# State updates of a gated linear attention, two chunks side by side in the row halves of the array

## The reference

```python
def step(S, inp):
    qn, kn, vn, gn = inp
    b = jnp.cumsum(gn, axis=1)
    b_last = b[:, -1]
    q_dec = qn * jnp.exp(b)
    k_inv = kn * jnp.exp(-b)
    attn = jnp.where(causal, jnp.einsum('bthd,bshd->bhts', q_dec, k_inv), 0.0)
    o = (jnp.einsum('bhts,bshv->bthv', attn, vn)
         + jnp.einsum('bthd,bhdv->bthv', q_dec, S))
    k_tail = kn * jnp.exp(b_last[:, None] - b)
    S = S * jnp.exp(b_last)[..., None] + jnp.einsum('bshd,bshv->bhdv', k_tail, vn)
    return S, o
```

## Time and profile before

| what | value |
|---|---|
| median of 3 runs | 4279.65 us (4272.71 to 4283.12) |
| the profiled execution | 4281.71 us |
| its span, first to last instruction | 4279.9 us |
| mean granted TensorE clock | 0.967 of full speed |
| the stage of the change, layer 0 and layer 1 | 116.98 and 113.94 us |

### The profile page before, as it was taken

One profiled execution on the slowest core, in us unless ns is written; L12 is line 12 of the kernel. 1 busy time (PEld: TensorE's weight loads), 2 busy tenths in 40 slices (PEclk: granted clock), 3 DMA queues, 4 the chain that ended last, 5 costly groups with the idle time before them and its releaser, 6 DMA issues.

```text
span 4279.9 us, 49995 instructions
## 1 busy us (share of the span) xinstructions
PE 4056.3 (95%) x18106; PEld 3279.2 (77%) x18106; DVE 2821.2 (66%) x4282; ACT 1530.1 (36%) x2219; POOL 1845.6 (43%) x956
## 2 busy tenths in 40 slices
PE   6899998998999999999998999989899999999999
PEld 4666876886877887888876668778778778788887
DVE  3124754698988946888733156247988989378786
ACT  2434523343333333333335255233333333333332
POOL 2321223344444446777423212333344444487772
PEclk9998989999999999999999998999999999999999
DMA  6434975243445459999934358463334544699996
GB/s 246 143 116 145 329 268 201 81 143 113 170 158 201 167 206 333 382 347 349 314 127 140 103 200 301 158 194 106 125 128 179 189 159 169 239 373 372 351 350 210
DMA packets 411891, 918.72 MB, mean 215 GB/s; under 512 B 38544, under 2 KB 176560, under 8 KB 410064
## 3 DMA queue, kind: packets, MB, share of 16 engines
q1 hardware_dynamic: 328080, 664.83, 44.8%
q0 software_dynamic: 45056, 134.38, 8.6%
q10 hardware_dynamic: 38592, 117.46, 7.0%
HBM read 793.85 MB, written 256.90 MB: 246 GB/s over the span
## 4 chain that ended last, share of the span: by engine, by line
PE 77%; issue 10%; DVE 6%; ACT 3%; POOL 3%; DMA 1%; SPq 1%; POOLq 0%; ACTq 0%; DVEq 0%
PE ps L887 13%; PE ps L888 13%; PE ps L889 13%; PE ps L902 10%; PE ps L903 10%; PE ps L904 10%; POOL w_lo L841 3%; PE ps L1185 2%; PE ps L1074 1%; PE ps L1059 1%; PE ps L1019 1%; DMA raw<-in_stream_dram 1%; ACT w_hi L519 1%; DVE raw L1263 1%; PE ps L1082 1%
## 5 line engine op out<-in xcount | busy, mean ns | idle before, releaser
L841 POOL TENSOR_TENSOR w_lo<-raw,w_hi 128x1024 fp32r<-128x1024 f32 x440 | 1133.5, 2577 | 2076.0 <-ACT w_hi L519 2076.0
L519 ACT ACTIVATE w_hi<-raw 128x1024 fp32r<-128x1024 f32 x504 | 534.2, 1060 | 1873.0 <-PE ps L889 1397.2
L887 PE MATMUL ps<-h_hi,w_hi 128*128 128x512 f32 x2880 | 1146.0, 398 | 7.9 <-DVE idxT L1522 7.8
L888 PE MATMUL ps<-h_hi,w_lo 128*128 128x512 f32 x2880 | 1137.3, 395 | 0.0
L889 PE MATMUL ps<-h_lo,w_hi 128*128 128x512 f32 x2880 | 1134.8, 394 | 0.0
L887 PEld LDWEIGHTS ps<-h_hi,w_hi 128*128 128x128 f32 x2880 | 550.3, 191 | 130.7 <-issue 17.4
L889 PEld LDWEIGHTS ps<-h_lo,w_hi 128*128 128x128 f32 x2880 | 547.8, 190 | 120.1
L888 PEld LDWEIGHTS ps<-h_hi,w_lo 128*128 128x128 f32 x2880 | 549.0, 191 | 107.9
L854 POOL DMA_INDIRECT down<-expert_down,e_row x256 | 336.3, 1314 | 216.6 <-DVE ps L1647 95.9
L1594 DVE TENSOR_TENSOR hot_i<-same_i,pick 128x1024 fp32r<-128x1024 f32 x192 | 421.5, 2195 | 0.0
L846 POOL DMA_INDIRECT acts<-expert_act,e_act x256 | 375.5, 1467 | 104.1 <-issue 77.4
(11 more groups left out here) (255 smaller groups left out, 6048.2 us busy)
## 6 DMA issues: line engine op xcount, KB each, us to landing
raw<-in_stream_dram SPq DMA_DIRECT2D x648, 512.0 KB, 3.4
expert_down<-in_stream_dram SPq DMA_DIRECT2D x256, 512.0 KB, 5.9
expert_act<-gel ACTq DMA_DIRECT2D x256, 256.0 KB, 2.0
raw_more<-in_stream_dram SPq DMA_DIRECT2D x128, 512.0 KB, 6.8
expert_gate<-gatebuf ACTq DMA_DIRECT2D x12, 4096.0 KB, 12.5
a_in<-expert_act SPq DMA_DIRECT2D x128, 384.0 KB, 6.6
g_in<-expert_gate SPq DMA_DIRECT2D x128, 384.0 KB, 8.2
ada_first<-in_stream_dram SPq DMA_DIRECT2D x16, 512.0 KB, 12.6
```

Source lines behind the costliest of these rows:

```text
L519: return act.activation(o, i, ACT.Copy)
L841: pool.tensor_tensor(w_lo[:, s, :], raw[:, b, :], w_hi[:, s, :].bitcast(F32), ALU.subtract).then_inc(lo_ready, 1)
L887: pe.matmul(o, w_hi[:, s, w], mov_hi[:, c, :], start=c == 0, stop=False)
L888: pe.matmul(o, w_lo[:, s, w], mov_hi[:, c, :], start=False, stop=False)
```

## The change

The updates of both chunks of a pair are made together, two heads at a time. The first half of a pair's updates (`half` 0) takes heads 0 and 1, the second heads 2 and 3. Within a half the order is head by head and, for each head, chunk `2 * p` in rows 0 to 63 and then chunk `2 * p + 1` in rows 64 to 127. The even chunk's products go to bank 4, the odd one's to bank 5. The last pair has only its even chunk. The unit stands between the two halves.

VectorE makes both halves before it waits for the squares. Since the odd chunk's state is now there before the pair's outputs have read the other two, a third state buffer is used, `state_2`, over the part of `grow` that is free in this stage.

```diff
+    state_2 = at("state_2", 88.5, [P, GH, DV])
...
+        def state_at(c, h):
+
+            return state[:, c % 3, h, :] if c % 3 < 2 else state_2[:, h, :]
...
+                def updates(l, p, half):
+                    n = l * 2 * TT + 2 * p + half
+                    if n:
+                        pe.wait_ge(state_ready, n)
+                    for h in (2 * half, 2 * half + 1):
+                        for e in range(2 if p < TT - 1 else 1):
+                            r = slice(64 * e, 64 * e + 64)
+                            mm = pe.matmul(ps[:, 4 + e, h % 2 * 256:h % 2 * 256 + 256], ktail[r, h, p, :],
+                                           v_g[r, p, h * DV:(h + 1) * DV], start=True, stop=True)
+                    mm.then_inc(upd_mm, 1)
...
-                    for e in range(2):
-                        c = 2 * p + e
-                        if e:
-                            unit(l, U_SQ + 3 * p)
-                        if c == 7:
-                            break
-                        if c:
-                            pe.wait_ge(state_ready, l * 7 + c)
-                        r = slice(64 * e, 64 * e + 64)
-                        for h in range(GH):
-                            mm = pe.matmul(ps[:, 4 + h // 2, h % 2 * 256:h % 2 * 256 + 256], ktail[r, h, p, :],
-                                           v_g[r, p, h * DV:(h + 1) * DV], start=True, stop=True)
-                        mm.then_inc(upd_mm, 1)
+                    updates(l, p, 0)
+                    unit(l, U_SQ + 3 * p)
+                    updates(l, p, 1)
...
-                    pe.wait_ge(state_ready, l * 7 + 2 * p + 1)
+                    pe.wait_ge(state_ready, l * 2 * TT + 2 * p + 2)
...
+                def update(p, half):
+                    dve.wait_ge(upd_mm, l * 2 * TT + 2 * p + half + 1)
+                    if p:
+                        dve.wait_ge(o_mm, l * TT + p)
+                    for e in range(2 if p < TT - 1 else 1):
+                        c = 2 * p + e
+                        for h in (2 * half, 2 * half + 1):
+                            u = ps[:, 4 + e, h % 2 * 256:h % 2 * 256 + 256]
+                            if c == 0:
+                                ins = dve.tensor_copy(state_at(1, h), u)
+                            else:
+                                ins = dve.scalar_tensor_tensor(out=state_at(c + 1, h), in0=state_at(c, h),
+                                                               scalar=small[:, 40 + h * 8 + c:41 + h * 8 + c], in1=u,
+                                                               op0=ALU.mult, op1=ALU.add)
+                        if e == 0 and p < TT - 1:
+                            step(ins)
                     ins.then_inc(state_ready, 1)
...
-                    update(2 * p)
+                    update(p, 0)
+                    update(p, 1)
                     dve.wait_ge(o_sq, l * 16 + 4 * (p + 1))
...
-                    if p < TT - 1:
-                        update(2 * p + 1)
```

More of the change, by code:

```diff
@@ L1033, in _ @@
                         if p:
-                            pe.matmul(o[0:64], q_g[:, h, t0:t0 + 64], state[:, 0, h, :], start=False, stop=False,
+                            pe.matmul(o[0:64], q_g[:, h, t0:t0 + 64], state_at(2 * p, h), start=False, stop=False,
                                       skip_group_check=True)
-                        mm = pe.matmul(o[64:128], q_g[:, h, t0 + 64:t0 + 128], state[:, 1, h, :], start=False, stop=True,
+                        mm = pe.matmul(o[64:128], q_g[:, h, t0 + 64:t0 + 128], state_at(2 * p + 1, h), start=False, stop=True,
                                        skip_group_check=True)
@@ L1323, in _ @@
                 mask = const[:, C_CAUSAL:C_CAUSAL + P].bitcast(U32).unsqueeze(1).to_broadcast([P, GH, P])
[L1325 to L1340, removed]
+                def update(p, half):
[14 more added lines that the diff above has]
+                            step(ins)
                     ins.then_inc(state_ready, 1)
-                    dve.wait_ge(state_ready, l * 7 + c + 1)
+                    dve.wait_ge(state_ready, l * 2 * TT + 2 * p + half + 1)
                 for p in range(TT):
```

## The result

| | median | lowest to highest |
|---|---|---|
| before, 4 runs | 4277.74 us | 4272.71 to 4283.12 |
| changed, 4 runs | 4244.95 us | 4239.61 to 4246.71 |

The ratio is 0.9921, with a 95% interval of 0.9904 to 0.9938: 32.8 us less by the medians, 26.5 to 41.1 by the interval. The forecast was 4242 us, 4234 to 4259. The profiled execution of the changed kernel took 4239.61 us, with a span of 4237.8 us, and is the fastest of its four; by the two spans the difference is 42.1 us. Which of these differences is the change's own is the first thing to settle, so I read the stretches before anything else.

What follows compares the result with a forecast made beforehand. TensorE's own row of work, waits included, was taken to bound the kernel. Waits and low clock 26.2, less 0.5 for added mode changes, plus 11.6 for row halves gave 37.3 us: 4279.65 to 4242 us, range 4234 to 4259.

Steps and rivals of the forecast that it cites:

- The waits and the low clock behind them: Before the first updates of pairs 1 to 3, both layers: 15.7 us waiting and 10.9 low clock go; 26.2 remain.
- No new wait in its place: At the second half of a pair's updates TensorE won't wait for VectorE; rival of a new wait: 4268 us, 0.06.
- the forecast margin at pair 1: VectorE done at 268.0, TensorE at the second half at 268.4: 0.4 us in time.
- Row halves side by side: Update blocks with two chunks take 0.96 instead of 1.92 us, 11.6 us in all; rival of serial halves: 4254 us, 0.16.
- The lower bound: In 12 update blocks the halves run serially, each of three alternations costing some 0.15 us: a loss of 5.4 us.
- The start of each stage: The first two-chunk block of each stage runs at the low clock; side by side saves 1.0 us each, 2.0 together.
- 26.2 - 0.5 + 7.7: The 0.5 us is added cost in both layers: pair 3's single update, split around a unit, enters and leaves 64-row mode again.
- Given back behind the stage: Rival: time saved is lost behind the stage, where DMA share is 0.94; up to all returns, 4279 us, chance 0.05.

Runs made afterwards that it cites:

- the order alone: Kernel before with a third state buffer and the odd chunk's update moved ahead of the wait for the squares, matmuls unchanged: 4258.0 us, ratio 0.9926.
- the cover away: Changed kernel with the projection unit moved from between the two update halves to behind them: 4295.59 us, ratio 1.002 to the kernel before.
- one alternation in the program: Changed kernel with both heads of the even chunk ahead of both of the odd one within a half: 4245.69 us, ratio 0.9897 to before.
- the later ones: Changed kernel unaltered, run twice more beside the kernel before: 4238.76 us (ratio 0.9883) and 4248.69 us (ratio 0.9899).
- the second set: Changed kernel unaltered, run again beside the kernel before: 4238.76 us against 4288.5, ratio 0.9883.
- the long wait: Changed kernel with TensorE also waiting for the previous pair's normalised outputs before the first updates of pairs 1 to 3: 4277.19 us, ratio 0.9971 to before.
- the short one: Changed kernel with TensorE waiting only for ScalarE's square root before the first updates of pairs 1 to 3: 4258.22 us, ratio 0.9938 to before.
- the unit moved ahead: Changed kernel with the stage's first projection unit moved ahead of the last key transposes: 4236.22 us (ratio 0.9887 to before), again 4241.32 us (0.989).

## Why the prediction was right, point by point

**The waits and the low clock behind them: 26.2 us forecast.** Right. They are gone in the trace, and the order alone, which does only this, takes 29.1 us off the stages. These are its starts, cut as above, and the rest of each stage:

```profile
229.23:244.67 15.44, 15.44 (x49) 11.62 (x49) 8.16 (x7) 1.97 (x3) 1.62 (x2) 0.67 0.37 127
2326.49:2338.12 11.63, 11.63 (x49) 9.15 (x49) 8.17 (x7) 2.14 (x3) 1.63 (x2) 0.90 0.48 170
244.67:332.03 87.36, 87.36 (x393) 62.78 (x393) 17.51 (x45) 22.02 (x48) 25.50 (x11) 1.00 0.35 121
2338.12:2425.48 87.36, 87.36 (x393) 62.79 (x393) 17.52 (x45) 22.02 (x48) 25.50 (x11) 1.00 0.35 121
```

The 2.9 us beyond the forecast lie for the most part at the start of layer 1, which took 11.63 us in that execution against 13.81 before: the low clock from the pause ahead of the stage ended sooner there.

**No new wait in its place: costed at nothing.** Right, and so was the margin. The terms that I wrote for VectorE (263.88, 1.58, 0.6, 1.66 and 0.1) add up to 267.8 and not to 268.0, so the forecast margin at pair 1 was 0.6 us and not 0.4. VectorE's first half of pair 1 in the changed kernel:

```profile
261.92 1.77 DVE L1343 SCALAR_TENSOR_TENSOR state<-state,small,ps 128x256 f32<-128x256 f32 x4
```

It ended at 263.7 us and TensorE came at 264.31, 0.6 us later. With the cover away the same dependence costs 49.7 us, the low clock included.

**Row halves side by side: 0.96 us a block, 9.6 us for ten, 2.0 for the first two.** The mechanism was right, the sizes were slightly off. A block takes 1.06 us instead of 0.96, so ten give 8.6. The overlap itself is complete: the first half of the last pair in the changed kernel has the even chunk alone, 4 records in one row half, and takes as long as 8 records in two:

```profile
306.88:307.94 1.06, 1.06 (x6) 0.67 (x5) 0.34 (x2) 0.59 (x4) 0.00 (x0) 1.00 0.93 332
```

Four records fewer in turn take 0.86 us less (1.92 to 1.06), so by my estimate each takes 0.215 and 0.2 us of a block belongs to its two ends. I had halved that as well. The experiments give 12.1 us with the order already right and 13.8 with the pauses kept, the starts of the stages included. Row halves overlap as column halves do, 1.92 to 1.06 or 1.8 times. The lower bound, that each alternation costs a change of mode, is out: with one alternation in the program the block takes 1.07 us, with three 1.06. That agrees with the Trainium skill, page "TensorEngine Tiling (Array Packing)", Key Properties, where tiles of one mode run in parallel and only a change of the mode drains the engine.

**The start of each stage.** This is the term that was mis-sized. I gave the two layers 2 us each (1.0 for the block at the low clock, 0.96 for the one at the high clock), 3.9 together. They gave 3.50 and 3.86 us, 7.4. I had assumed that the clock comes back at the same moment as before. It came back sooner, at 235.4 instead of 240.0 us in layer 0, and in layer 1 inside the first block. From the first scores to that moment, first before and then changed:

```profile
229.50:239.98 10.48, 10.48 (x28) 7.99 (x29) 8.16 (x7) 0.43 (x1) 1.02 (x1) 0.51 0.54 188
2345.30:2352.83 7.53, 7.53 (x22) 5.62 (x23) 7.14 (x7) 0.43 (x1) 0.00 (x0) 0.55 0.52 184
228.87:235.38 6.51, 6.51 (x22) 4.98 (x23) 6.15 (x2) 0.43 (x1) 1.04 (x1) 0.50 0.85 298
2322.07:2324.34 2.27, 2.27 (x10) 2.05 (x12) 2.19 (x1) 0.60 (x1) 1.03 (x1) 0.50 0.99 365
```

By these clocks some 17 us of the two starts ran at the low level before and 8.8 now. Half of the difference, about 4.1 us, is time saved, and 3.3 of the 7.4 are left for the four blocks. From the second block on the forecast was 33.4 us (26.2 - 0.5 + 7.7 for eight blocks), and the traces have 101.58 + 100.13 - 168.42 = 33.3. So the 3.4 us by which 40.6 exceeds 37.3 lie at the two starts. Why the clock came back sooner I can't tell: in the kernel with the order alone it did so in layer 1 with blocks of full length, and not in layer 0. With one profiled execution of the kernel before it also stays open how much of the 4.1 us the change would give every time.

**Given back behind the stage: 0.05.** It was not; 4047.5 us outside the stages against 4049.0. The later executions with 4054.9 and 4069.3 can't be compared with a trace of before of their own; there the medians speak.

**The total.** 32.8 us by the first medians, 49.7 and 38.4 by the later ones, 40.6 in the stages. The forecast of 37.3 stands among them, though below the interval of the second set (42.0 to 58.3). Its closeness owes something to chance. From the second block on two errors cancel: the order alone gives 27.0 us there (201.71 less twice 87.36) where 26.2 stood, and eight blocks give 6.9 where 7.7 did.

## What to carry to other kernels

If an engine pauses for a result, look first whether the engine that makes it could have made it before its own wait: here that order, and one more buffer, was worth 29 of 41 us, and the packing of the array 12, of which 12 blocks of 0.86 us explain 10. A pause on TensorE of 2 to 5 us cost about 2 us again in low clock nearly every time, so short waits are worth more than their length. And if a dependence is split in two halves, the work put between them is part of the change: without it the same change gained nothing.

## What the runs showed of the hardware that was not expected

- Two matmuls in different row halves overlap whether the program has them as neighbours or two matmuls apart: 1.06 and 1.07 us for a block of 8 records, against 1.92 for 8 in one row half. The second row half is free: 4 records in one half alone take 1.06 us too.
- Pauses of 1.29 us left the clock at 1.00 at pair 2 and brought the low level at pair 3, in both layers. Of 22 pauses from 2.1 to 5.6 us (six in the kernel before, six with the long wait, two with the short one, eight without cover) 21 brought it; one of 2.99 us did not. The kernel with the unit moved ahead had two more: 2.75 us brought it, 1.13 us did not. The price of one that did was 1.8 us in the kernel before (10.9 for six), 2.4 with the long wait (11.8 for five) and 1.8 without cover (49.7 less 35.3 us of pauses, for eight).
